# Small sums and the meta rows' values on column tiles of the matmul array; the latent ranks' inverse spread by 32-row products

## The reference, cut to what matters

```python
def rms_norm(x, g):
    y = xf * lax.rsqrt(jnp.mean(xf * xf, axis=-1, keepdims=True) + EPS)
...
    q = to_heads(rms_norm(c_q, q_norm) @ w_uq, MLA_HEADS)      # rank 256
    kv = to_heads(rms_norm(c_kv, kv_norm) @ w_ukv, MLA_HEADS)  # rank 128
...
    y_ret = from_heads(head_rms(retention(rq, rk, rv)))
    y_mla = from_heads(head_rms(y_mla)) * mla_out_gain[layer]
```

## Time and profile before

| | us |
|---|---|
| three executions | 1494.06, 1495.54, 1497.20 |
| median | 1495.54 |
| the profiled execution, its time | 1495.57 |
| the profiled execution, its span | 1493.7 |
| PE busy in the span | 1479.8 |
| DVE, ACT busy | 1225.9, 1011.2 |

### The profile page before, as it was taken

How to read it: one execution, slowest core, us unless ns; L and a number is a source line. 1 busy time by engine, 2 the same in 40 slices (tenths; PEclk the granted TensorE clock), 3 DMA queues, 4 the chain that set the end, 5 groups by cost and what they waited for, 6 DMA issues and landing times.

```text
span 1493.7 us, 21688 instructions
## 1 busy us (share of the span) xinstructions
PE 1479.8 (99%) x8276; PEld 1284.9 (86%) x8276; DVE 1225.9 (82%) x1040; ACT 1011.2 (68%) x947; POOL 48.3 (3%) x71
## 2 busy tenths in 40 slices
PE   9999999999999999999999999999999999999998
PEld 9879999999988988888888888888888888888886
DVE  7747777777875688888889898998899888988887
ACT  8656433333675577777777777777777777777775
POOL 0000000000000040000000000000000000000000
PEclk9999999999999999999999999999999999999999
DMA  9306544444422579999999999989999999999992
GB/s 365 144 14 242 198 170 169 170 170 170 157 104 103 198 291 412 379 355 408 369 359 407 381 348 404 382 342 400 382 359 388 402 376 353 406 373 345 422 387 115
DMA packets 65289, 445.08 MB, mean 298 GB/s; under 512 B 8185, under 2 KB 8473, under 8 KB 13392
## 3 DMA queue, kind: packets, MB, share of 16 engines
q1 hardware_dynamic: 60912, 433.15, 74.3%
q0 software_dynamic: 3456, 9.72, 2.3%
q10 hardware_dynamic: 864, 1.40, 0.3%
HBM read 439.28 MB, written 7.37 MB: 299 GB/s over the span
## 4 chain that ended last, share of the span: by engine, by line
PE 95%; DVE 2%; ACT 1%; DMA 1%; issue 1%; DVEq 0%; ACTq 0%
PE bank L548 93%; PE bank L552 3%; DMA hT<-h 1%; DVE w_lo L1384 0%; DVE sq L1539 0%; ACT scratch L1127 0%; ACT scratch L1128 0%; ACT L1116 0%; DVE w_lo L1710 0%; DVE parts L1398 0%; ACT w_hi L1050 0%; DVEq L1756 0%; ACT scratch L1125 0%; ACT scratch L1109 0%; DVE hT L1576 0%
## 5 line engine op out<-in xcount | busy, mean ns | idle before, releaser
L548 PE MATMUL bank<-w_hi,parts 128*128 128x512 f32 x2688 | 725.4, 391 | 0.2 <-DVE w_lo L1710 0.2
L1710 DVE TENSOR_TENSOR w_lo<-ring,w_hi 128x2048 fp32r<-128x2048 f32 x285 | 653.1, 2292 | 85.5 <-ACT w_hi L1278 74.9
L1278 ACT ACTIVATE w_hi<-ring 128x2048 fp32r<-128x2048 f32 x285 | 547.0, 1919 | 168.3 <-PE bank L548 139.5
L548 PEld LDWEIGHTS bank<-w_hi,parts 128*128 128x128 f32 x2688 | 500.3, 188 | 101.9 <-DVE w_lo L1710 0.6
L548 PE MATMUL bank<-parts,w_hi 128*128 128x272 f32 (+1 forms) x2240 | 429.0, 290 | 1.1 <-DVE parts L1398 0.7
L548 PE MATMUL bank<-w_lo,parts 128*128 128x512 f32 x1344 | 415.0, 389 | 0.0
L548 PEld LDWEIGHTS bank<-parts,w_hi 128*128 128x128 f32 x2240 | 352.6, 189 | 4.5 <-issue 2.5
L548 PE MATMUL bank<-parts,w_lo 128*128 128x272 f32 (+1 forms) x1120 | 321.7, 287 | 0.0
L548 PEld LDWEIGHTS bank<-w_lo,parts 128*128 128x128 f32 x1344 | 252.3, 188 | 53.1
L548 PEld LDWEIGHTS bank<-parts,w_lo 128*128 128x128 f32 x1120 | 211.4, 189 | 0.2
L1050 ACT ACTIVATE w_hi<-ring 128x2048 fp32r<-128x2048 f32 x71 | 135.4, 1912 | 91.8 <-PE bank L548 91.7
(11 more groups left out here) (198 smaller groups left out, 620.9 us busy)
## 6 DMA issues: line engine op xcount, KB each, us to landing
ring<-stream SPq DMA_DIRECT2D x356, 1024.0 KB, 6.6
hT<-stream SPq DMA_DIRECT2D x48, 1024.0 KB, 6.8
ring<-stream SPq DMA_DIRECT2D x4, 512.0 KB, 8.9
ring<-stream SPq DMA_DIRECT2D x2, 976.0 KB, 4.6
ring<-stream SPq DMA_DIRECT2D x2, 768.0 KB, 10.4
c_sb<-consts SPq DMA_DIRECT2D x1, 1136.0 KB, 16.2
hT<-h ACTq DMA_DIRECT2D x4, 272.0 KB, 7.3
ring<-stream SPq DMA_DIRECT2D x4, 256.0 KB, 5.9
```

The source lines that it names most:

```text
L548: return release(nc.tensor.matmul(dst, lhsT, rhs, start=start, stop=stop), inc)
L1278: A(w_hi[:, n % HSLOTS, :], moe_slot(m), ACT.Copy).then_inc(split_hi, 1)
L1710: V.tensor_tensor(w_lo[:, n % HSLOTS, :], moe_slot(m), w_hi[:, n % HSLOTS, :].bitcast(F32), ALU.subtract).then_inc(split_lo, 1)
```

## The change

1. `sM` and `sR`: each of the four products now uses 32 columns of ones and writes only its own 32 partitions, one column tile for each head. The constant `C_PACK` goes.
2. `v2`: four products of 32 tokens by 128 value columns, one column tile for each head, instead of one of 16 tokens by 512. The values of head h stand on partitions 32h to 32h+15; the weights of the meta tokens go to the same partitions of one tile (`meta_probs`), and `yM` reads both there.
3. The latent sums: three products on two column tiles (partitions 0 to 31 for the key rank, 32 to 63 for the query rank). Scale, epsilon, root and reciprocal work on 64 partitions by 272 columns. Two new products over 32 rows, `bc0` and `bc1`, spread the two inverses to 128 partitions; PE makes them between the projections `k1` and `k2`, and ACT copies them out after `k1`. `latent_norm` on DVE moves from before `rope(3)` to behind `rope(6)`.

```diff
-OUTS = (["ckv", "kpe", "cq0", "cq1", "q0", "q1", "sckv", "scq", "q2", "q3", "k0", "k1", "k2", "k3",
+OUTS = (["ckv", "kpe", "cq0", "cq1", "q0", "q1", "sc", "q2", "q3", "k0", "k1", "bc0", "bc1", "k2", "k3",
...
-                def ones_sum(name, srcs):
-                    dst = rot_bank(name)
-                    for i, x in enumerate(srcs):
-                        mm(dst, ones, x, i == 0, i == len(srcs) - 1, out_done if i == len(srcs) - 1 else None)
+                def latent_sums():
+                    dst = rot_bank("sc")
+                    pe.wait_ge(out_free, o_("cq1", layer) + 1)
+                    mm(dst[0:32, :], ones[:, 0:32], sq3[:, 0, :], True, True)
+                    mm(dst[32:64, :], ones[:, 0:32], sq3[:, 1, :], True, False)
+                    mm(dst[32:64, :], ones[:, 0:32], sq3[:, 2, :], False, True, out_done)
+
+                def latent_spread(i):
+                    dst = rot_bank(f"bc{i}")
+                    pe.wait_ge(c_inverse, layer + 1)
+                    x = slice(32 * i, 32 * i + 32)
+                    mm(dst, col(C_ROW + i * P)[x, :], std[x, 0, :], True, True, out_done)
...
-                    if u < HEADS:
-                        mm(dst, vals[0:META, 2, c], STy[0:META, b, f0:L], True, False)
-                    else:
-                        m = slice(32 * h, 32 * h + META)
-                        mm(dst, meta_rv[m, :], meta_decayed[m, f0:L], True, False)
+                    m = slice(32 * h, 32 * h + META)
+                    values, weights = (meta_vm, meta_probs) if u < HEADS else (meta_rv, meta_decayed)
+                    mm(dst, values[m, :], weights[m, f0:L], True, False)
...
-                        mm(dst, col(C_PACK + 96 - 32 * h), sq3[:, 2 * h + odd, f0:L], h == 0, h == HEADS - 1,
+                        mm(dst[32 * h:32 * h + 32, :], ones[:, 0:32], sq3[:, 2 * h + odd, f0:L], True, True,
                            out_done if h == HEADS - 1 else None)
...
-                pe.wait_ge(out_free, o_("cq1", layer) + 1)
-                ones_sum("sckv", [sq3[:, 0, :]])
-                ones_sum("scq", [sq3[:, 1, :], sq3[:, 2, :]])
+                latent_sums()
                 for r, name in enumerate(ROPES[3:9], start=2):
+                    if name == "k2":
+                        latent_spread(0)
+                        latent_spread(1)
                     proj(name, 2 + r // 2, r % 2)
...
-                for t in range(3):
-                    dst = rot_bank(f"v{t}", 512)[0:TILES[t][1], :]
-                    mm(dst, tok_rows(ckv, t), w[:, 512:1024], True, True, out_done)
+                for t in range(2):
+                    mm(rot_bank(f"v{t}", 512), tok_rows(ckv, t), w[:, 512:1024], True, True, out_done)
+                dst = rot_bank("v2", P)
+                for h in range(HEADS):
+                    mm(dst[32 * h:32 * h + 32, :], ckv[:, 0:32], w[:, 512 + h * P:512 + (h + 1) * P], True, True,
+                       out_done if h == HEADS - 1 else None)
...
-                def mean(name, dst, n):
-                    A(dst, src(name), ACT.Copy, scale=1.0 / n).then_inc(out_free, 1)
+                def means(name):
+                    s = src(name)
+                    A(std[0:32, 0, :], s[0:32, :], ACT.Copy, scale=1.0 / KVR)
+                    A(std[32:64, 0, :], s[32:64, :], ACT.Copy, scale=1.0 / QR).then_inc(out_free, 1)
...
-                    A(STy[0:META, h % 2, f0:L], y[0:META, f0:L], ACT.Copy).then_inc(pt_free, 1)
+                    A(meta_probs[32 * h:32 * h + META, f0:L], y[0:META, f0:L], ACT.Copy).then_inc(pt_free, 1)
...
-                        A(std[:, 0:2, :], std[:, 0:2, :], ACT.Sqrt).then_inc(mean_rooted, 1)
+                        A(std[0:64, 0, :], std[0:64, 0, :], ACT.Sqrt).then_inc(mean_rooted, 1)
...
+                    if name == "k1":
+                        keep("bc0", std[:, 1, :])
+                        keep("bc1", std[:, 2, :])
...
-                for t, (_, rows) in enumerate(TILES):
-                    keep(f"v{t}", vm[0:rows, t, :], rows, 512)
+                for t in range(2):
+                    keep(f"v{t}", vm[:, t, :], P, 512)
+                keep("v2", meta_vm, P, P)
...
-                    dve.wait_ge(mean_rooted, layer + 1)
-                    link(V.reciprocal(std[:, 0:2, :], std[:, 0:2, :]))
-                    for x, g, s in [(ckv, G_KV + layer, 0), (cq[:, 0, :], G_Q + 2 * layer, 1), (cq[:, 1, :], G_Q + 2 * layer + 1, 1)]:
+                    dve.wait_ge(out_free, o_("bc1", layer) + 1)
+                    for x, g, s in [(ckv, G_KV + layer, 1), (cq[:, 0, :], G_Q + 2 * layer, 2), (cq[:, 1, :], G_Q + 2 * layer + 1, 2)]:
...
                 low(b + 5)
-                latent_norm()
+                dve.wait_ge(mean_rooted, layer + 1)
+                V.reciprocal(std[0:64, 0, :], std[0:64, 0, :]).then_inc(c_inverse, 1)
                 rope(3)
                 rope(4)
...
                 rope(6)
+                latent_norm()
                 rope(7)
```

More of the change, by code:

```diff
@@ L88 @@
 C_LOW = C_IOTA + CAP
-C_PACK = C_LOW + EXPERTS * EXPERTS
-C_ROW = C_PACK + 7 * P // 4
+C_ROW = C_LOW + EXPERTS * EXPERTS
 C_COLS = C_ROW + HEADS * P
 TILES = [(META, P), (META + P, P), (0, META)]
-OUTS = (["ckv", "kpe", "cq0", "cq1", "q0", "q1", "sckv", "scq", "q2", "q3", "k0", "k1", "k2", "k3",
+OUTS = (["ckv", "kpe", "cq0", "cq1", "q0", "q1", "sc", "q2", "q3", "k0", "k1", "bc0", "bc1", "k2", "k3",
          "qn0", "qn1", "qpe0", "qn2", "qpe1", "qn3", "kn0", "kn1", "kn2", "kn3", "v0", "v1", "v2",
@@ L223, in build @@
         meta_rv, meta_decayed = rv[:, 2, 0:P], rv[:, 2, P:P + L]
+        meta_vm, meta_probs = vm[:, 2, 0:P], STy[:, 0, :]
         at[0] = 0
@@ L277, in build @@
         rot_ready, rope_done = sem("rot_ready"), sem("rope_done")
-        c_ready = sem("c_ready")
+        c_ready, c_inverse = sem("c_ready"), sem("c_inverse")
         sc_done, sc_free, p1_ready, exp_done, p2_ready = (
@@ L336, in first_of @@
         def first_of(name, layer):
-            return META if layer and name[0] in "qgysb" and name not in ("sckv", "scq") else 0
+            return META if layer and name[0] in "qgysb" and name[:2] != "bc" and name not in ("sc",) else 0
         def base_of(layer):
@@ L1156, in attention @@
                 keep_raw("q1")
-                mean("sckv", std[:, 0, :], KVR)
-                mean("scq", std[:, 1, :], QR)
+                means("sc")
                 high(b + 5)
@@ L1507, in attention @@
                 dve.wait_ge(eps_ready, layer + 1)
-                dve.wait_ge(out_free, o_("scq", layer) + 1)
-                V.tensor_tensor(std[:, 0:2, :], std[:, 0:2, :], std[:, 2:3, :].to_broadcast([P, 2, L]), ALU.add).then_inc(mean_ready, 1)
+                dve.wait_ge(out_free, o_("sc", layer) + 1)
+                V.tensor_tensor(std[0:64, 0, :], std[0:64, 0, :], std[0:64, 2, :], ALU.add).then_inc(mean_ready, 1)
                 low(b + 5)
-                latent_norm()
+                dve.wait_ge(mean_rooted, layer + 1)
+                V.reciprocal(std[0:64, 0, :], std[0:64, 0, :]).then_inc(c_inverse, 1)
                 rope(3)
@@ L1803, in _tables @@
     c[:, C_IOTA:C_IOTA + CAP] = np.arange(CAP)
-    c[:, C_LOW:C_PACK] = np.tril(np.ones((EXPERTS, EXPERTS)), -1).ravel()
-    c[:, C_PACK + 96:C_PACK + P] = 1.0
+    c[:, C_LOW:C_ROW] = np.tril(np.ones((EXPERTS, EXPERTS)), -1).ravel()
     for h in range(HEADS):
```

## The result

The changed kernel takes 1497.55 us (median of 22 executions, 1492.36 to 1498.75). The kernel before takes 1494.24 us in the same series, also 22 executions. The medians lie 3.3 us apart (0.22%). The ratio taken over the executions is 1.0015, 95% interval 1.0009 to 1.0021. The forecast was 1493.9, within 1491.3 to 1497.2. So the change is a small loss where a small gain was forecast, and the measured median lies above the range.

A forecast was written before the change was run, and what follows sets the result against it. The prediction took PE to bound the kernel, busy 1479.8 of 1493.7 us. Its terms, -2.00 (sR) + 0 (sM) - 1.22 (v2) - 0.22 (latent sums) + 1.76 (spreads) = -1.68, took 1495.57 to 1493.9 us, range 1491.3 to 1497.2.

The forecast's parts named there:

- Latent sums: PE's latent sums: 1.39 us instead of 1.50, a gain of 0.11 a layer, 0.22 us for both.
- spreads: New PE products bc0 and bc1 between k1 and k2: 0.88 us a layer, 1.76 us lost.
- v2: Values product on PE: 0.36 us instead of 0.97, a gain of 0.61 twice, 1.22 us.
- sR: Head sums ahead of wo: 0.93 us instead of 1.96, gaining 1.03 and 0.97, together 2.00 us.
- sM's gain is absorbed before yR2: About 1.0 us a layer won at sM becomes PE waiting before yR2, since ACT's table load holds the root; counted as nothing.
- the gain of sM is kept: Rival at sM: the root moves, its table load hidden or started earlier; 1491.9 us, chance 0.08.
- The clock: Likeliest case, as summed: PE waits 1.0 us longer before yR2 with the clock as before; 1493.9 us, chance 0.51.
- The rival that named it: Around yR2, PE's longer wait and narrow products bring extra half-clock stretches of 3.4 us, each costing 1.7 us.
- one more stretch: Clock rival's case of one extra half-clock stretch near yR2: 1495.6 us, no change; chance 0.18.
- two or more: Clock rival's case of extra half-clock stretches in both layers: 1497.3 us with two, slower than before; chance 0.06.
- The base of the sum: Whole program: the profiled execution's 1495.57 us, taken as 0.03 above the median of the runs shown, without a shift.
- tiles that run one after another: Rival at sums, v2 and spreads: column tiles do not overlap; +4.0 us, 1499.5 us, chance 0.02.

The follow-up runs named there:

- early_table: Changed kernel, with ACT taking a root of a small tile behind its copies of yM2, so the root's table loads there: 1491.34 us, ratio 0.9972.
- narrow_plus: Kernel before, with sM on column tiles and one product of ones by ones ahead of the wait for decay(2): 1496.24 us, ratio 1.0013.
- sR alone: Kernel before with one edit, sR on column tiles: median 1492.18 us.
- half_sM: Kernel before, with sM making only two of its four full products, heads 0 and 3: 1497.8 us, ratio 1.0022.
- sM alone: Kernel before with one edit, sM on column tiles: 1500.28 us, ratio 1.0034.
- one_sM: Kernel before, with sM making only one of its four full products, head 0: 1499.73 us, ratio 1.0030.

## Why the prediction was wrong

- **Latent sums, spreads, v2, sR: right.** Forecast for a layer were a gain of 0.11, a cost of 0.88, a gain of 0.61 and 0.93 us for the shortened sR; layer 0 of the trace has 0.14, 0.86, 0.62 and 0.93. The parts run alone give the same sums to 0.1 us. bc0 and qn0 wait for nothing: latent_norm ends at 45.68 (forecast 45.5), qn0 starts at 48.51.
- **sM's gain is absorbed before yR2: right.** yR2 in layer 0 is 0.46 us later than before, exactly as late as ACT's table load and root (102.07 for 101.61, 103.37 for 102.91) and as the scores behind v2. The load and not sM sets the root, as early_table showed. The rival "the gain of sM is kept" needed the root to move, which early_table brought about.
- **The clock: this step failed.** The sum put sM at nothing: the microsecond won becomes a microsecond of waiting before yR2, and that wait was free, "with the clock as before". The wait came as forecast (1.36 us for about 1.4), but it cost PE its clock: 13.65 us at half clock in the profiled execution, some 6.0 us, and 4 us or more in 20 of 22 executions. With sM full again, or with the wait filled, the cost was gone (1492.33 and 1492.34).
- **The rival that named it was too small.** It had the place, the mechanism and the sign. It took the one stretch of the earlier trace rows as the size of any stretch, 3.4 us at a price of 1.7; the new ones in the profile are 6.83 us each. That could hardly be seen: layer 0 had none before and layer 1 only one to read. It gave one more stretch 0.18 and "two or more" 0.06, though the prediction itself had found that PE's wait would be longer by a microsecond in both layers. Its reading of the earlier trace rows is also off by a line: the 14 records ran inside the half-clock stretch, and the window ahead of it has 17, with PE idle for 0.43 of 3.50 us.
- **The base of the sum.** The sum was made against 1495.57, an execution with a half-clock stretch in layer 1. In the result's series 17 of 22 executions of the kernel before lie at 1493.82 to 1494.60, where none shows by the time, and the median came out at 1494.24. So the base was 1.3 us above the median. The sum of the parts was -1.68, and 1494.2 - 1.7 = 1492.5 is what the undisturbed executions show.
- **What the stretches cost.** From the 1492.4 us without them to the profiled 1498.4 it is 6.0 us for 13.65 us at half clock, so 0.44 us for each, where the prediction took 0.5. At that price a short stretch costs 1.5 us and a long one 3.0. The changed kernel's middle group lies 4.1 to 4.9 us up, which would be one of each; that is an estimate, since no trace shows an execution of it. Ledger: 2.77 us in layer 0 (1.73 plus sR's 1.04), and 1.56 us in layer 1 on top of what before's own stretch cost, which is about 1.5 (the kernel before's two groups, 1494.2 and 1495.6).
- **A rival's sum is off.** For tiles that run one after another the prediction has v2 cost 0.2 us. By its own price eight passes of 0.11 are 0.88 us against the 0.97 of before, so a gain of 0.2 for the two layers, and its 1499.5 would be about 1499.1. Nothing hangs on it: the tiles overlapped.

The Trainium skill, "TensorE: Matmul & The Clock Gate", Part 1, says in effect that the gate's resting state is the throttled one and that activity is what lifts it. The filler run agrees with the second half: with 1.5 us of useless products in the wait of layer 0 and as many in layer 1, the clock stayed at 1.00 through both attention parts of the profiled execution.

## What to carry to other kernels

Shortening work on TensorE ahead of a wait that another engine ends gives nothing and can cost several times the saving in granted clock (here 2.0 us of work saved, some 6 us lost in the profiled execution); so move the wait's release first (here one line, decay(2) ahead of a reciprocal), and only then shorten. Where the wait can't be moved, fill it with products into an empty bank. When executions of a kernel fall into groups by granted clock, price edits group by group, since the median moves with the share of the groups.

## What the runs showed of the hardware that was not expected

- A half-clock stretch in the attention parts had one of two lengths. It was 3.41 us in the kernel before, early_table and narrow_plus (layer 1) and in sR alone and half_sM (layer 0). It was 6.83 us in the changed kernel, sM alone and one_sM (both layers). No third length came there in any of the 16 profiles.
- It comes or not in executions of one and the same program, and a loss of 4 us or more grew more frequent with waits of 1.05, 1.24, 1.36 and 1.70 us (3 of 12, 6 of 12, 26 of 28, 6 of 6).
- The table load costs 1.28 us, and the root starts 1.30 us after the load does. The Trainium skill, "ScalarE: Activation LUTs", What ACT_TABLE_LOAD costs, has the same 1283 ns for the load but about 1.38 us of drain on top; in this trace none shows between the copy at 101.67 (0.39 us), the load at 102.07 and the root at 103.37, and the measurement decides.
- Expected, and shown for both sums in both layers: column tiles with four different moving operands overlap. sM's eight narrow passes of 272 columns take 0.60 us (101.26 to 101.86), where its eight full ones took 1.84 (100.71 to 102.55).
